# The last expert's down weights fetched in two pieces, with two gate units ahead of the second-last down product

## What is computed

```
for e in range(N_EXPERTS):
    he = jax.nn.silu(t @ w_gate[e]) * (t @ w_up[e])
    out = out + gates[:, e:e + 1] * (he @ w_down[e])
...
x = x + (g2 * ffn).astype(x.dtype)
return _rmsnorm(x, p['final_norm_g']), ...
```

## Time and profile before

| what | us |
|---|---|
| median of three executions | 851.9 |
| lowest and highest of the three | 851.34, 852.39 |
| profiled execution, its time | 854.28 |
| its span, from the first to the last instruction | 852.7 |

### The profile page before, as it was taken

The page is one execution under the profiler, slowest core; times in us unless marked ns, Lnnn a source line. Parts: engine busy times, 40 slices in busy tenths (PEclk is TensorE's granted clock), DMA queues, the critical chain, the costliest instruction groups (busy, mean ns, idle before and its releaser), DMA issues.

```text
span 852.7 us, 13557 instructions
## 1 busy us (share of the span) xinstructions
PE 777.3 (91%) x4188; PEld 585.8 (69%) x4189; DVE 583.7 (68%) x743; ACT 480.2 (56%) x540; POOL 88.3 (10%) x143
## 2 busy tenths in 40 slices
PE   2799999999999999579996789999999999999967
PEld 0477777778787878258872577777777778777523
DVE  1375564747455564774668678778888878888687
ACT  5324464545364554670453657677777767777503
POOL 3000202111111202120003100000000000000350
PEclk9999999999999999899997989999999999999989
DMA  8928093957758391910008998758999999997563
GB/s 315 347 106 273 26 349 108 322 129 270 200 199 267 134 337 64 329 49 4 1 1 322 379 393 350 277 201 322 377 389 389 401 395 385 402 397 281 173 247 123
DMA packets 94826, 213.85 MB, mean 251 GB/s; under 512 B 4618, under 2 KB 55882, under 8 KB 88659
## 3 DMA queue, kind: packets, MB, share of 16 engines
q1 hardware_dynamic: 89476, 194.16, 62.8%
q0 software_dynamic: 2880, 10.49, 3.3%
q10 hardware_dynamic: 2448, 8.91, 2.6%
HBM read 181.56 MB, written 44.56 MB: 265 GB/s over the span
## 4 chain that ended last, share of the span: by engine, by line
PE 80%; DMA 7%; DVE 6%; ACT 3%; issue 2%; SPq 2%; POOL 1%; DVEq 0%; ACTq 0%; POOLq 0%
PE z L1156 39%; PE fill_ps L1866 17%; PE z L1866 11%; PE z L1120 5%; DMA ada_w<-in_ada_w 2%; PE z L1254 2%; PE fill_ps L1783 2%; DMA ada_w<-in_sb_w_o 2%; DMA exp_w<-in_exp_w_down 1%; SPq L1405 1%; PE fill_ps L1789 1%; PE fill_ps L1285 1%; DMA w_pair<-in_sb_w_qkv 1%; DMA slots_out<-y_slot 1%; PE fill_ps L1156 1%
## 5 line engine op out<-in xcount | busy, mean ns | idle before, releaser
L527 DVE TENSOR_TENSOR w_lo<-exp_w,w_hi 128x1024 fp32r<-128x1024 f32 x192 | 223.4, 1220 | 52.7 <-ACT w_hi L523 52.6
L523 ACT ACTIVATE w_hi<-exp_w 128x1024 fp32r (+1 forms) x192 | 196.4, 1055 | 71.3 <-PE z L1156 48.2
L1156 PE MATMUL z<-w_hi,x_slotT_hi 128*128 128x512 f32 x288 | 124.1, 431 | 8.3 <-DVE x_slotT_lo L944 4.7
L1156 PE MATMUL z<-w_hi,x_slotT_lo 128*128 128x512 f32 x288 | 115.3, 400 | 0.0
L1156 PE MATMUL z<-w_lo,x_slotT_hi 128*128 128x512 f32 x288 | 114.7, 398 | 0.0
L1866 PE MATMUL fill_ps<-h_hi,wp_hi 128*128 128x512 f32 x192 | 78.3, 408 | 1.5 <-DVE h_lo L1637 1.5
L1866 PE MATMUL fill_ps<-h_lo,wp_hi 128*128 128x512 f32 x192 | 77.1, 401 | 0.0
L1866 PE MATMUL fill_ps<-h_hi,wp_lo 128*128 128x512 f32 x192 | 76.3, 397 | 0.0
L1156 PEld LDWEIGHTS z<-w_hi,x_slotT_hi 128*128 128x128 f32 x288 | 55.1, 191 | 25.2 <-issue 8.8
L1156 PEld LDWEIGHTS z<-w_lo,x_slotT_hi 128*128 128x128 f32 x288 | 55.2, 192 | 15.5 <-issue 3.8
L1156 PEld LDWEIGHTS z<-w_hi,x_slotT_lo 128*128 128x128 f32 x288 | 54.8, 190 | 13.4
(11 more groups left out here) (344 smaller groups left out, 1488.8 us busy)
## 6 DMA issues: line engine op xcount, KB each, us to landing
exp_w<-in_exp_w_gate SPq DMA_DIRECT2D x18, 2048.0 KB
exp_w<-in_exp_w_up SPq DMA_DIRECT2D x18, 2048.0 KB
exp_w<-in_exp_w_down SPq DMA_DIRECT2D x18, 2048.0 KB
ada_w<-in_ada_w SPq DMA_DIRECT2D x12, 2048.0 KB, 9.3
slots_in<-zeros SPq DMA_DIRECT2D x7, 2048.0 KB, 12.8
w_pair<-in_sb_w_qkv SPq DMA_DIRECT2D x24, 512.0 KB, 5.6
slots_out<-y_slot ACTq DMA_DIRECT2D x17, 512.0 KB, 10.1
x_slot<-slots_in SPq DMA_DIRECT2D x16, 512.0 KB, 10.0
```

The lines of the kernel that those rows point to most:

```text
L523: act.activation(w_hi[:, u % RING, :].unsqueeze(1), raw_unit(b, u), ACT.Copy).then_inc(hi_ready, 1)
L527: dve.tensor_tensor(w_lo[:, u % RING, :].unsqueeze(1), raw_unit(b, u), w_hi[:, u % RING, :].bitcast(F32).unsqueeze(1), ALU.subtract).then_ ...
L1156: return pe.matmul(out, lhsT, rhs, start=start, stop=stop, skip_group_check=True)
```

## The change

Four places change. SP fetches the last expert's down weights in two DMAs: blocks 0 to 2 as soon as DVE has split the three blocks of slot m-1 that lay there, block 3 when the product of slot m-1 is done; it waits for the store of slot m no more. The second fetch has a semaphore of its own, for which PE waits ahead of `out(m + 1)`. PE multiplies two gate units instead of one ahead of `out(m)`. ACT splits two up units instead of one ahead of the copy of slot m's product. DVE splits two up units ahead of the first gated tile, and takes the fifth gated tile behind the hidden rows of slot m+1.

```diff
+    last_down_loaded = sem("last_down_loaded")
...
         before = next_of(m, -1)
-        sp.wait_ge(down_ready, m)
-        sp.nop(nofuse=True)
-        sp.wait_ge(y_slot_stored, 16 * (m + 2))
+        sp.wait_ge(lo_ready, units_before(m) + 2 * RING + KS)
         sp.nop(nofuse=True)
         sp.wait_ge(exp_loaded[2], 16 * (m + 1))
         sp.nop(nofuse=True)
-        load_expert(sp, 2, before[0], before[0] % 2, before[1])
+        load_down(sp, *before, range(0, KS), exp_loaded[2])
+        sp.wait_ge(down_ready, m)
+        sp.nop(nofuse=True)
+        load_down(sp, *before, range(KS, KF), last_down_loaded)
...
+    def load_down(sp, e, cond, ks, done):
+        dst = exp_w[:, bass.ds(e % 2, 1), 8192 + ks[0] * D:8192 + ks[0] * D + len(ks) * D].rearrange("p b (k f) -> p b k f", f=D)
+        src = io["exp_w_down"][0].rearrange("e (p k) f -> p e k f", p=P)
+        sp.dma_start(dst, src[:, bass.ds(e, 1), ks[0]:ks[0] + len(ks)], cond=cond).then_inc(done, 16)
...
             hi_unit(act, b, RING + u)
-            if u == 0:
+            if u == 1:
                 keep_y(m)
...
         keep_hidT(m)
-        rest_of_up(m + 1, range(1))
+        rest_of_up(m + 1, range(2))
         for i in range(2):
             gated_y(early_y, TILES[i], 0, early_step)
-        rest_of_up(m + 1, range(1, 3))
+        rest_of_up(m + 1, range(2, 3))
         gated_y(early_y, TILES[2], 0, early_step)
         rest_of_up(m + 1, range(3, RING))
         gate_by_sig(m + 1)
-        for i in range(3, NT):
-            gated_y(early_y, TILES[i], 0, early_step)
+        gated_y(early_y, TILES[3], 0, early_step)
         keep_hid(m + 1)
         keep_hidT(m + 1)
+        gated_y(early_y, TILES[4], 0, early_step)
...
-        half_in(m + 1, 0, range(1))
+        half_in(m + 1, 0, range(2))
         out(m)
-        half_in(m + 1, 0, range(1, RING))
+        half_in(m + 1, 0, range(2, RING))
         half_in(m + 1, 1)
         turn_hid(m + 1)
+        pe.wait_ge(last_down_loaded, 16)
         out(m + 1)
```

## The result

| | median, us | range, us | executions |
|---|---|---|---|
| before | 851.88 | 850.49 to 854.09 | 8 |
| after | 857.75 | 854.14 to 859.91 | 8 |

The ratio is 1.0068, with a 95% interval of 1.0052 to 1.0083: 4.4 to 7.1 us slower. The forecast was 852.9, with a range up to 854.8. The profiled execution took 859.91 us, the slowest of the eight, with a span of 858.1.

What follows compares the result with a forecast made beforehand. It took two chains of almost equal length to bound the end: the late fetch, and store, gathers and DVE's late tiles. DVE's copy -1.0, half group -0.2 and clock +2.2 made 851.9 + 1.0 = 852.9 us; range 849.6 to 854.8.

Steps and rivals of the forecast that it cites:

- Whom the fetch meets: Early fetch against the store of slot m-1: the store, early gathers and DVE's chain shift by 0.4 us, bounds 0 to 2.
- s: The shift of the store of slot m-1, and with it the early gathers and DVE's chain; taken as 0.4 us.
- the forecast's first sign: First of the signs listed as showing the forecast: SP's two early fetches land before 797 us.
- its sign of being wrong: At POOL's gathers: the prediction is wrong if they start late by more than 1 us.
- the fetch delays the store: Rival, chance 0.16: the store of slot m-1 lands behind what lies ahead; with a 2 us shift, 854.5 us.
- its +1.0 us: Net change at the kernel's end: DVE's copy -1.0, PE's saved half group -0.2, the clock +2.2.
- The fetch: SP's two early fetches of the last down weights: landing by 797.8 and 801.9, costing nothing, with 12 us of cover.
- The extra units: Second gate unit on PE and second up unit on DVE fall into idle gaps; slot m's product shifts about 0.2 us.
- DVE from the early tiles on: DVE's chain after the early gathers: `hidT` at 813.9, last product ending near 822, but DVE's copy only at 829.0.
- The eight microseconds: The last product ends 8 us earlier, but DVE isn't ready, since its tiles and POOL's additions run one after the other.
- The tail: PE after the last product: resumes at 830.4, gains 1.2 us, loses 2.2 to the lower clock, ends at 847.4.

Runs made afterwards that it cites:

- e4: The changed kernel with block 3's fetch held back until the store of slot m-1 has landed; ratio to before 1.0028.
- all five runs: The changed kernel, e1, and the changed kernel with block 3 halved, cut to 8 columns, or blocks 0 to 2 fetched singly; ratios 1.0004 to 1.0068.
- e2: The kernel before with only the new order of PE, ACT and DVE, keeping the old single fetch; ratio to before 1.0005.
- e3: The changed kernel with both early fetches cut to 8 columns, so all waits but almost no bytes; ratio to before 1.0000.
- e12: e4 with POOL's second and third early additions moved to DVE and four unread products in PE's gap; 849.47 us, ratio to before 0.9973.
- e1: The kernel before with only SP's two early fetches and PE's wait, in the old order; 855.48 us, ratio to before 1.0037.
- e5: e4 with four products that nobody reads added in PE's gap; 851.24 us, ratio to before 0.9989.

## Why the prediction was wrong

**The step that failed is "Whom the fetch meets".** It shifted the store of slot m-1 by s = 0.4 us, with bounds of 0 to 2; s was 5.8 - 2.7 = 3.1. Two things went wrong in it. The fetch was taken to move 410 GB/s from about 789, so that all was through by 794.1. It was issued as forecast, but for 0.2 us (789.00 instead of 787.9, T0 itself being 0.9 later); yet the first 2 us with data moved 264 GB/s, not 410, so at the store's issue 0.75 MB were still to move. And the store was taken to lose at most the time of such bytes at the full rate, 0.8 MB in 2 us. It waited for block 3 to land instead, which happened at 798.5, and landed 1.2 us behind it: 3.1 us lost. The bound on the bytes was right, their price was too small. That both fetches land before 797, the forecast's first sign, failed by this, and its sign of being wrong, gathers that start over 1 us late, came. The rival "the fetch delays the store" had the mechanism; the bound of 2 us, which it shared, was too small. That the forecast had the direction right says little: its +1.0 us came from DVE's copy and the tail, as in e4, and most of the measured loss from the store.

The Trainium skill (DMA: Bandwidth & Descriptors, section Queues, rings and completion order) has the engines go round robin between queue rows, packet by packet, from which the forecast took that the store could lose at most its own 1.3 us. The measured 3.1 us are more, so by this case that rule doesn't bound the delay. The same section has the semaphore's increment land only after every earlier write of the same DMA engine. The store's landing behind block 3's in all five runs agrees with that; the size comes from when block 3 landed.

**The rest of the loss.** With s = 3.1 the forecast's own working, 1.6 us for s = 2, gives 2.7 us on top of its +1.0: 3.7 at PE's end. Measured were 4.7. Of the missing 1.0 us, 0.6 lie ahead of DVE's copy (42.75, where 39.4 + 2.7 = 42.1 stood). There DVE waited 0.83 us for the hidden rows (816.73): the late gated tiles pushed back a split unit, PE stood idle for 3.57 us until 811.83, and the clock was 0.63 from 812 to 814. The other 0.4 lie in the tail, 18.8 us from DVE's copy to PE's end (852.05 - 833.25), where the forecast had 847.4 - 829.0 = 18.4. The medians lie 5.9 us apart; the 0.9 us of T0 are no effect that any run ties to the change.

**"The fetch" and "The extra units"** were right in what they claim of themselves: PE didn't wait for the fetch, and e2 shows that the order alone costs nothing.

**"DVE from the early tiles on"** held. Where the store isn't delayed, `hidT` comes at 23.95 us (e3) and 24.51 (e4), forecast 813.9 - 789.59 = 24.3, and the copy at 38.26 and 38.81, forecast 39.4. In the changed kernel a tile of DVE took 6.08 us and ended 1.09 us behind POOL's two additions (819.21 + 4.65 = 823.86), as in the earlier trace rows; the last product ended at 828.18 and DVE's copy came at 833.25. The eight microseconds went where the forecast had them go; e3 shows it most directly, since without the fetch's bytes, and with the store on time, no time is gained. Two details were wrong and cost nothing. Before, DVE's third late tile ended 0.62 us ahead of the last product's end (829.28 and 829.90), not 0.72. And the last product, forecast with 7.14 us at clock 1.00, took 8.77, with the clock at its lower level in the middle:

```profile
820.00:822.00 2.00, 2.00 (x3) 0.67 (x2) 2.00 (x1) 0.00 (x0) 2.00 (x2) 0.50 0.76 262
```

**"The tail"** held: PE stood idle for 4.46 us and then ran at 0.50, and in e12, without the gap, the clock stayed at 1.00 there. PE took 852.05 - 834.61 = 17.4 us to its end, where 14.8 + 2.2 = 17.0 stood, so the clock cost some 2.6 us, above its bounds of 1.6 to 2.2.

Three things stay open: why block 3 needs 5.7 us for 0.5 MB; why the medians of e1 and of the change differ when their traces don't; and e5's gain, which is larger than its trace shows. Single profiled executions and medians differ by up to 3.8 us here (e1's took 859.31 against its median of 855.48, before's own 854.28 against 851.9), and that bounds what the table can tell.

## What to carry to other kernels

A transfer that is moved into an idle stretch of the DMA engines must be through before the next store on which others wait: ask when its last bytes land, and don't count from its issue at the full rate. Here the first 2 us were slow, and the last 0.5 MB landed 5.7 us after their issue. When one of two chains of nearly equal length is shortened, only the difference is gained; here only a kernel in which DVE's chain was shortened too and PE's gap was filled (e12) beat the one before by its interval. Time that PE spent waiting came back here as a lower clock in what followed, so look where a stall that is moved takes its clock loss.

## What was unexpected of the hardware

- A small store (0.5 MB) behind a fetch on another engine's queue landed 1.2 to 1.3 us after the fetch's last piece: 2.7, 3.9 and 5.8 us from its issue with 0, 0.26 and 0.52 MB in a DMA issued 1.1 us ahead. 1.5 MB that had been issued 5 us ahead cost it 0.1 us (e4).
- 0.5 MB that followed 1.5 MB on the same queue took 5.7 us to land, and the 0.07 MB of fetch and store that began to move last took some 2.3 us.
- PE's clock fell in e5 while PE was busy again after a gap of 2 us: 0.56 and 0.58 in the two stretches from 830 to 834.
